# First MLP of a three-layer hybrid block: 17 of 22 pairs of up-projection tiles by seven block products

## The chip, the cores and the metric

One NeuronCore of a Trainium2 chip runs the whole program in one launch. The metric is the device time of an execution in microseconds (us); three runs of the kernel before gave 1718.68, 1718.99 and 1719.04 us, median 1718.99.

## What is computed

The reference runs a hybrid layer (gated linear attention beside sliding-window attention, then an MLP) and then two further layers, each an attention and an MLP, on 512 tokens of width 1024, in float32. The change touches the MLP of the first layer alone:

```
h2 = rms_norm(x, ffn_norm)                       # 512 x 1024
u = causal_dwconv(h2 @ w_up, conv_w, conv_b)     # w_up 1024 x 5632, three taps along the tokens
a, bval = jnp.split(u, 2, axis=-1)               # 2816 columns each
return x + (jax.nn.silu(a) * bval) @ w_down      # w_down 2816 x 1024
```

## The kernel before

Activations lie transposed: 128 features on the partitions, 512 tokens along the free axis. Every float32 product is made of three passes in a rounded format (fp32r): a value is split into a rounded "hi" (a copy by ACT) and the remainder "lo" (a subtraction), and hi x hi, hi x lo and lo x hi are summed in PSUM.

The up projection has 22 pairs of output tiles. A pair is one 128-column tile of `a` (p_ = 0) and its partner of `bval` (p_ = 1). A tile (`up_tile`, lines 1027 to 1038) is 8 chunks of the inner dimension by 3 passes, 24 matmuls of 128x512. Weights come by SyncE's queue as 128x1024 tiles into `stage`; ACT writes `w_hi` (`split_hi`, line 1506), GpSimd (POOL) writes `w_lo` in four operations of 128x256 (`split_lo`, line 507); each has two buffers. The evacuation of a tile runs on DVE and ACT in turn: DVE scales the bank by `rstd` (L2445), ACT starts the convolution (L1767), DVE adds the two other taps (L2447, L2450); after the first tile of a pair ACT takes the silu (L1770), after the second DVE multiplies (L2455) and the result is split at once into `f1_hi` (ACT, L1772) and `f1_lo` (DVE, L2458). The pairs rotate over four banks. The down projection (L1080 to L1086) then runs over `d`, the eight output tiles, each over all 22 tiles `f` in order; it reads `f1_hi` and `f1_lo` from the arena, which holds all 44 of them.

The later MLPs do their down projection already by seven products (`product`, L1444 to L1453) for each 2x2 group of weight blocks, a "quad": raw blocks land by DMA, ACT makes the hi parts (L2031), POOL and DVE the lo parts (L549, L2848), DVE the sums of weight blocks (L2830 to L2842) and the additions of the products (L2890). A product is 4 chunks by 3 passes, 12 matmuls of 128x256.

Each engine works its own program in order; a waiting instruction holds all that stand behind it. Orders are written out by hand.

Of the kernel before, what the change touches and what calls it, by code (L numbers as in the profile page):

```python
# [21 lines left out]
P = 128  # L22
# [28 lines left out]
N_UP1 = 2 * NF1  # L51
# [33 lines left out]
N_FC = 2 * KD * N_CH  # L85

# [46 lines left out]
def program(nc, x_in, params, consts, buckets, swa_table, weights, pairs, tables, out):  # L133
    with ExitStack() as ctx:
# [15 lines left out]
        with nc.sbuf_tensor("y", [P, 2, KD, HS], F32) as y:  # L150
            pass
        xn_hi = sb("xn_hi", [P, KD, S], F32R)
# [4 lines left out]
        with nc.sbuf_tensor("ff_space", [P, 2 * KD, S], F32) as early_space:  # L157
            with nc.sbuf_tensor("z", [P, N_IN, S], F32) as z, nc.sbuf_tensor("qkv", [P, 2, 3, S], F32) as qkv, \
                    nc.sbuf_tensor("prob", [P, 2, 2, S], F32) as prob, \
                    nc.sbuf_tensor("v_tok", [P, 2, 2, NQ, P], F32) as v_tok:  # L160
                pass
        arena = sb("arena", [P, 2 * NF1, S], F32R)
        v_split = sb("v_split", [P, 2, 2, NQ, P], F32R)
        bias = sb("bias", [P, 2, 2, EXT])
        tmp = sb("tmp", [P, 4, S])
        rstd = sb("rstd", [P, S])
        rstd_h = sb("rstd_h", [P, S])
# [10 lines left out]
        f1_hi, f1_lo = arena[:, 0:NF1], arena[:, NF1:2 * NF1]  # L178
# [81 lines left out]
        up_scaled, down_done = sem("up_scaled"), sem("down_done")  # L260
# [64 lines left out]
        flat_bias = bias[:].rearrange("p a b c -> p (a b c)")  # L325
# [55 lines left out]
        def _(sp):  # L381
# [15 lines left out]
            def quad_load(q, r):  # L397

                if q >= 2:
                    sp.wait_ge(slot_low, 5 * (q - 2) + (LO_POOL[HI_S4] if r == 0 else LO_POOL[HI_A22]))  # L400
                sp.dma_start(quad_in[q % 2][r], pairs[2 * q + r]).then_inc(quad_full[q % 2], 16)

            def mlp2_loads(l):

                for n in range(N_CH):
                    t = T_MLP2[l] + KD * n
                    q = quad_at(l, n)
                    if n:
# [16 lines left out]
                if l == 0:  # L425
                    sp.wait_ge(slot_low, 5 * quad_at(1, 0))
# [46 lines left out]
            loads(T_MLP1 + 4, T_QKV[0])  # L473
# [27 lines left out]
        def _(pool):  # L501
# [44 lines left out]
            def quad_low(q, k, src):  # L546

                pool.wait_ge(slot_high, N_HIGH * q + k + 2)
# [43 lines left out]
            split_los(T_OUT + 6, T_MLP2[0])  # L592
# [47 lines left out]
        def _(pe):  # L640
# [386 lines left out]
            def up_tile(m, p_, bank, first=False):  # L1027

                pe.wait_ge(hi_ready, 2 * m + p_ + 1)
                for k in range(KD):  # L1030
                    if first:
                        pe.wait_ge(xn_ready, KD + k + 1)
                    pe.matmul(UP[bank][:], w_hi[:, p_, k], xn_hi[:, k], start=(k == 0), stop=False)  # L1033
                    mm = pe.matmul(UP[bank][:], w_hi[:, p_, k], xn_lo[:, k], start=False, stop=False)  # L1034
                mm.then_inc(hi_free, 1)
                pe.wait_ge(lo_ready, 2 * m + p_ + 1)
                for k in range(KD):
                    mm = pe.matmul(UP[bank][:], w_lo[:, p_, k], xn_hi[:, k], start=False, stop=(k == KD - 1))  # L1038
                mm.then_inc(tile_done, 1)

            m = T_MLP1 // 2
            pe.wait_ge(evac[0], m + WO_HALVES)
            up_tile(m, 0, 0, first=True)
# [5 lines left out]
            pe.wait_ge(evac[1], m + WO_HALVES)  # L1049
            up_tile(m, 1, 1)  # L1050
            up_tile(m + 1, 0, 2)
            up_tile(m + 1, 1, 3)
            with pe.Fori(1, NF1 // 2) as i:
                for j in range(2):
                    pe.wait_ge(ff_ready, 2 * i + j - 1)
                    up_tile(2 * i + (m + j), 0, 2 * j)
                    pe.wait_ge(conv_2, 4 * i + (2 * j - 2))
                    up_tile(2 * i + (m + j), 1, 2 * j + 1)

            for d in range(KD):  # L1060
# [6 lines left out]
                if d < 2:  # L1067
                    pe.wait_ge(ff_ready, NF1 - 1)
                    pe.wait_ge(conv_2, 2 * NF1 - 2)
                else:  # L1070
                    pe.wait_ge(evac[d % 2], T_MLP1 // 2 + WO_HALVES + d // 2)
                for s_, ks in pieces:
# [4 lines left out]
                    for k, f in ks:  # L1077
                        if d == 0 and f == NF1 - 1:
                            pe.wait_ge(ff_ready, NF1)
                        pe.matmul(G[d % 2][:], w_hi[:, p_, k], f1_hi[:, f], start=(f == 0), stop=False)  # L1080
                        mm = pe.matmul(G[d % 2][:], w_hi[:, p_, k], f1_lo[:, f], start=False, stop=False)  # L1081
# [2087 lines left out]
```

## Time and profile before

| | |
|---|---|
| median of the runs shown | 1718.99 us |
| the profiled execution's own time | 1718.6 us |
| its span in the trace | 1716.8 us |
| TensorE (PE) busy | 1704.7 us, 99% |
| DVE / ACT / POOL busy | 1061.0 / 868.3 / 963.1 us |
| granted TensorE clock | 0.999 |
| up projection, tile (1,0) to the first matmul of the down projection | 210.15 to 438.63 us |

Busy time is the time in which an engine's records run. Records of matmuls overlap, since they are pipelined, so the start-to-start distance is what one of them costs. On DVE, ACT and POOL too a record can end up to 0.1 us after the next one has begun; who waits for it by a semaphore waits for its end.

### The profile page before, as it was taken

The numbers are of one execution on the slowest core, as the hardware profiler recorded it, in microseconds if no ns is written. First come the engines' busy times: TensorE is split into PE (matmuls) and PEld (weight loads), VectorE is DVE, ScalarE is ACT, GpSimd is POOL, SyncE is SP. The second block draws the span as 40 slices with busy tenths as digits, with TensorE's granted clock in tenths as the row PEclk, the third lists the DMA queues.
The fourth block names the chain that finished last, engine by engine and source line by source line (L and its number), as shares of the span: only waits on it lengthen the run. The fifth ranks groups of instructions, "written<-read, shape, count | busy, mean of one in ns | idle before, by whom it ended". The sixth has DMA issues, their size and how long they took to land.

```text
span 1716.8 us, 27243 instructions
## 1 busy us (share of the span) xinstructions
PE 1704.7 (99%) x9425; PEld 1440.6 (84%) x9425; DVE 1061.0 (62%) x2084; ACT 868.3 (51%) x1498; POOL 963.1 (56%) x1095
## 2 busy tenths in 40 slices
PE   9999999999999999999999999999999999999998
PEld 7778888888888778888989898977777889898988
DVE  6875755555311455568757575867776676757576
ACT  5665555555322444435545444546655554545355
POOL 5543655555555434357666666755554665656666
PEclk9999999999999999999999999999999999999999
DMA  5221333332334322223323323233322242333332
GB/s 192 74 68 61 100 98 98 97 93 93 108 95 137 104 68 83 74 74 123 99 98 99 105 96 106 64 128 116 105 97 70 87 133 91 109 99 98 99 98 74
DMA packets 48662, 167.91 MB, mean 98 GB/s; under 512 B 5376, under 2 KB 6672, under 8 KB 48528
## 3 DMA queue, kind: packets, MB, share of 16 engines
q1 hardware_dynamic: 48272, 166.05, 30.2%
q8 instruction: 61, 1.00, 0.2%
q10 hardware_dynamic: 288, 0.52, 0.1%
q14 instruction: 41, 0.34, 0.1%
HBM read 164.31 MB, written 2.24 MB: 97 GB/s over the span
## 4 chain that ended last, share of the span: by engine, by line
PE 90%; DVE 6%; ACT 2%; issue 1%; DMA 0%; POOL 0%; SPq 0%; DVEq 0%; ACTq 0%
PE bank L736 18%; PE bank L1444 6%; PE bank L1453 6%; PE bank L1445 6%; PE bank L661 5%; PE bank L660 5%; PE bank L666 5%; PE bank L1033 5%; PE bank L1034 5%; PE bank L1038 5%; PE bank L754 3%; PE bank L760 3%; PE bank L755 3%; PE bank L1086 2%; PE bank L1081 2%; PE bank L1080 2%
## 5 line engine op out<-in xcount | busy, mean ns | idle before, releaser
L507 POOL TENSOR_TENSOR w_lo<-stage,w_hi 128x256 fp32r<-128x256 f32 x872 | 672.2, 803 | 571.7 <-ACT w_hi L1506 317.5
L1506 ACT ACTIVATE w_hi<-stage 128x1024 fp32r<-128x1024 f32 x218 | 229.4, 1052 | 200.9 <-PE bank L1081 54.7
L660 PE MATMUL bank<-xn_hi,w_hi 128*128 128x512 f32 x544 | 211.8, 389 | 0.0
L661 PE MATMUL bank<-xn_lo,w_hi 128*128 128x512 f32 x544 | 211.7, 389 | 0.0
L736 PE MATMUL bank<-xn_hi,w_hi 128*128 128x512 f32 x464 | 189.1, 407 | 0.0
L736 PE MATMUL bank<-xn_lo,w_hi 128*128 128x512 f32 x464 | 181.8, 392 | 0.0
L2890 DVE TENSOR_TENSOR x<-x,bank 128x256 f32<-128x256 f32 (+1 forms) x217 | 97.4, 455 | 89.3 <-PE bank L1453 86.6
L1453 PE MATMUL bank<-arena 128*128 128x256 f32 x896 | 146.6, 283 | 0.0
L1033 PE MATMUL bank<-xn_hi,w_hi 128*128 128x512 f32 x352 | 137.1, 389 | 0.0
L1034 PE MATMUL bank<-xn_lo,w_hi 128*128 128x512 f32 x352 | 136.9, 389 | 0.0
L666 PE MATMUL bank<-xn_hi,w_lo 128*128 128x512 f32 x544 | 135.0, 389 | 0.0
L1444 PE MATMUL bank<-arena 128*128 128x256 f32 x512 | 129.4, 284 | 1.3 <-DVE arena L2910 0.8
L1445 PE MATMUL bank<-arena 128*128 128x256 f32 x512 | 128.7, 283 | 0.0
L1453 PEld LDWEIGHTS bank<-arena 128*128 128x128 f32 x896 | 124.8, 192 | 0.0
L736 PE MATMUL bank<-xn_hi,w_lo 128*128 128x512 f32 x464 | 123.9, 399 | 0.0
L666 PEld LDWEIGHTS bank<-xn_hi,w_lo 128*128 128x128 f32 x544 | 102.1, 188 | 21.2
L661 PEld LDWEIGHTS bank<-xn_lo,w_hi 128*128 128x128 f32 x544 | 102.2, 188 | 21.1
L660 PEld LDWEIGHTS bank<-xn_hi,w_hi 128*128 128x128 f32 x544 | 102.1, 188 | 20.9
L2910 DVE TENSOR_TENSOR arena<-tmp,arena 128x256 fp32r<-128x256 f32 (+2 forms) x128 | 115.0, 917 | 3.8 <-ACT arena L2067 2.5
L736 PEld LDWEIGHTS bank<-xn_hi,w_hi 128*128 128x128 f32 x464 | 87.2, 188 | 25.2 <-issue 8.5
L736 PEld LDWEIGHTS bank<-xn_hi,w_lo 128*128 128x128 f32 x464 | 84.6, 188 | 22.8 <-issue 6.0
L736 PEld LDWEIGHTS bank<-xn_lo,w_hi 128*128 128x128 f32 x464 | 87.3, 188 | 16.0
(374 smaller groups left out, 3719.3 us busy)
## 6 DMA issues: line engine op xcount, KB each, us to landing
stage<-weights SPq DMA_DIRECT2D x219, 512.0 KB, 3.6
prob<-pairs SPq DMA_DIRECT2D x32, 512.0 KB, 3.6
stage<-pairs SPq DMA_DIRECT2D x32, 512.0 KB, 3.6
bias<-table SPq DMA_DIRECT2D x11, 896.0 KB, 6.4
out<-y SPq DMA_DIRECT2D x8, 256.0 KB, 2.2
x<-x_in SPq DMA_DIRECT2D x3, 512.0 KB, 7.6
bias<-swa_table SPq DMA_DIRECT2D x4, 256.0 KB, 4.4
con<-consts SPq DMA_DIRECT2D x1, 640.0 KB, 9.8
```

The costliest lines, as they stand in the source:

```text
L507: ins = nc.gpsimd.tensor_tensor(w_lo[:, p_, ks], stage[:, p_, ks], w_hi[:, p_, ks].bitcast(F32), ALU.subtract)
L660: pe.matmul(G[p_][:], w_hi[:, p_, k], hi[:, k], start=(first and k == ks[0]), stop=False)
L661: mm = pe.matmul(G[p_][:], w_hi[:, p_, k], lo[:, k], start=False, stop=False)
L666: mm = pe.matmul(G[p_][:], w_lo[:, p_, k], hi[:, k], start=False, stop=(last and k == ks[-1]))
L736: mm = pe.matmul(G[p_][:], (w_hi if i < 2 * KD else w_lo)[:, p_, k], (xn_lo if i < 2 * KD and i % 2 else xn_hi)[:, k], start=(i == 0), sto ...
L1033: pe.matmul(UP[bank][:], w_hi[:, p_, k], xn_hi[:, k], start=(k == 0), stop=False)
L1034: mm = pe.matmul(UP[bank][:], w_hi[:, p_, k], xn_lo[:, k], start=False, stop=False)
L1444: pe.matmul(region, w, fc_hi[:, i, f], start=(fresh and i == 0), stop=False, skip_group_check=True)
L1445: pe.matmul(region, w, fc_lo[:, i, f], start=False, stop=False, skip_group_check=True)
L1453: mm = pe.matmul(region, w, fc_hi[:, i, f], start=False, stop=(i == QUADS - 1), skip_group_check=True)
L1506: act.activation(w_hi[:, p_], stage[:, p_], ACT.Copy).then_inc(hi_ready, 1)
L2910: dve.tensor_tensor(fc_lo[:, i, a:b + 1].rearrange("p c s -> p (c s)"), src, fc_hi[:, i, a:b + 1].rearrange("p c s -> p (c s)").bitcast(F3 ...
```

## The change

The first 5 pairs stay as they are (`up_tile`). For the other 17, the two output tiles and the halves of the inner dimension make a 2x2 group of weight blocks A11, A12, A21, A22, and the halves of the inner dimension by the halves of the tokens a 2x2 group of activation blocks B. Seven products of sums of blocks give the pair: 7 x 12 matmuls of 128x256 in place of 2 x 24 of 128x512. The raw blocks of a pair come by two DMAs of 512 KB.

The 28 factor blocks (7 sums of B, for 4 chunks of the inner dimension, hi and lo) are made once, in four steps `factors(k)`, one after the first tile of each of the pairs 0 to 3. They take the arena's upper part. So the products f of the MLP (`f1`) stay unsplit in the lower part, and `f1_hi` and `f1_lo` are made at the end, when a factor's space is free. The multiplication `silu * b` moves from DVE to POOL. What was an ACT/DVE loop with register-indexed columns is written out.

```diff
@@ sizes
-N_UP1 = 2 * NF1
+N_PLAIN = 5
+Q_UP = NF1 - N_PLAIN
+UP_ORDER = [HI_A11, HI_S1, HI_A12, HI_S2, HI_S4, HI_A22, HI_S3]
+POOL_LOWS = [2, 5, 8, 11, 14, 17, 20]
+DVE_LOWS = [f for f in range(NF1) if f not in POOL_LOWS]
@@ POOL
+            for i in range(N_PLAIN - 1):
+                if i:
+                    f_made_of(i - 1)
+                split_lo(T_MLP1 // 2 + i + 1, 0)
+                factor_lows(i)
+                split_lo(T_MLP1 // 2 + i + 1, 1)
+            f_made_of(N_PLAIN - 2)
...
+            for q in range(Q_UP):
+                up_low(HI_S3, q)
...
+                    up_low(HI_A11, q + 1)
+                f_made_of(N_PLAIN + q - 1)
+                if q + 1 < Q_UP:
+                    for k in (HI_A12, HI_S4, HI_A22):
+                        up_low(k, q + 1)
+            split_lo(T_DOWN1 // 2, 0)
+            split_lo(T_DOWN1 // 2, 1)
+            f_low(POOL_LOWS[0])
+            f_low(POOL_LOWS[1])
+            f_made_of(NF1 - 1)
@@ TensorE, up_product(q, k)
...
+                elif k == HI_S2:
+                    pe.wait_ge(up_moved, moved_at(q, P1_COPY))
+                elif k == HI_S4:
+                    pe.wait_ge(up_moved, moved_at(q, P5_COPY))
@@ ACT
+            for i in range(N_PLAIN - 1):
+                split_hi(T_MLP1 // 2 + i + 1, 0)
+                conv_0_of(i, 0)
+                silu(i)
+                factor_highs(i)
+                split_hi(T_MLP1 // 2 + i + 1, 1)
+                conv_0_of(i, 1)
...
+            for q in range(Q_UP):
...
+                    u3_copied(q - 1)
+                silu(i - 1)
+                up_high(HI_S3, q)
+                p1_copied(q)
+                conv_0_of(i - 1, 1)
...
+                    up_high(HI_A11, q + 1)
...
+                p5_copied(q)
+                if more:
+                    up_high(HI_S1, q + 1)
+                    up_high(HI_A12, q + 1)
...
+                u2_copied(q)
+                if more:
+                    up_high(HI_S2, q + 1)
+                    up_high(HI_S4, q + 1)
...
+                conv_0_of(i, 0)
+                if more:
+                    up_high(HI_A22, q + 1)
@@ DVE
+            def factors(k):
+                dve.scalar_tensor_tensor(out=e[:, 0:S], in0=x[:, k], scalar=pcol("ffn_norm", k, k + 1), in1=rstd[:],
+                                         op0=ALU.mult, op1=ALU.mult)
+                dlink(dve.scalar_tensor_tensor(out=e[:, S:2 * S], in0=x[:, k + 4], scalar=pcol("ffn_norm", k + 4, k + 5), in1=rstd[:],
+                                               op0=ALU.mult, op1=ALU.mult))
+                dve.tensor_tensor(t1, b12, b11, ALU.subtract)
+                dlink(dve.tensor_tensor(t3, b22, b12, ALU.subtract))
+                dlink(dve.tensor_tensor(t2, b22, t1, ALU.subtract))
+                dve.tensor_tensor(t4, b21, t2, ALU.subtract).then_inc(factor_made, 1)
...
+                    ins = dve.tensor_tensor(SUM_Y[:], a2[:, 0:S], a2[:, S:], ALU.add)
...
+                    ins = dve.tensor_tensor(up_s3(q), a1[:, 0:S], a2[:, 0:S], ALU.subtract)
...
+            for i in range(N_PLAIN):
+                scaled(i, 0)
+                conv(i, 0)
+                if i < N_PLAIN - 1:
+                    factors(i)
+                    scaled(i, 1)
+                    conv(i, 1)
...
+            for q in range(Q_UP):
...
+                    c_1(q - 1)
...
+                if more:
+                    up_sum(q + 1, HI_S1)
+                    up_sum(q + 1, HI_S3)
+                    up_sum(q + 1, HI_S2)
+                conv(i - 1, 1)
+                c_00(q)
+                if more:
+                    up_sum(q + 1, HI_S4)
+                    up_sum_low(q + 1, HI_S1)
+                    up_sum_low(q + 1, HI_S2)
+                c_01(q)
+                conv(i, 0)
+            for f in DVE_LOWS[0:2]:
+                f_low(f)
+            c_1(Q_UP - 1)
+            conv(NF1 - 1, 1)
+            for f in DVE_LOWS[2:]:
+                f_low(f)
```

Helpers that the diff calls: `factor_highs(k)` on ACT makes the hi parts of a step's factors (one operation of 256, one of 1536 elements), `factor_lows(k)` on POOL the lo parts of four of them (one operation of 1024), DVE those of the other three (256 and 512). `c_00`, `c_01`, `c_1` on DVE add two products into half a bank each; `p1_copied`, `p5_copied`, `u2_copied`, `u3_copied` on ACT copy a product of 128x256 out of PSUM before TensorE adds to its region or writes it anew.

## Rows read from the trace of the kernel before

**Rows 1.** The profile's first page: span, busy time, and the chain that ended last.
```profile
span 1716.8 us, 27243 instructions
PE 1704.7 (99%) x9425; PEld 1440.6 (84%) x9425; DVE 1061.0 (62%) x2084; ACT 868.3 (51%) x1498; POOL 963.1 (56%) x1095
...
PE 90%; DVE 6%; ACT 2%; issue 1%; DMA 0%; POOL 0%; SPq 0%; DVEq 0%; ACTq 0%
```

**Rows 2.** Windows: stretch and length, busy us of each engine (records), clock, DMA.
```profile
210.10:438.60 228.50, 228.50 (x1009) 189.20 (x1009) 119.59 (x168) 125.16 (x148) 119.12 (x169) 1.00 0.31 97
834.60:865.00 30.40, 30.40 (x256) 30.40 (x255) 19.32 (x37) 13.85 (x24) 18.14 (x15) 1.00 0.33 105
```

**Rows 3.** Timeline of PE, up projection: start, us, engine, line, operands, count.
```profile
210.15 0.39 PE L1033 MATMUL bank<-xn_hi,w_hi 128*128 128x512 f32 x1
...
431.37 1.98 PE L1038 MATMUL bank<-xn_hi,w_lo 128*128 128x512 f32 x8
433.19 0.39 PE L1033 MATMUL bank<-xn_hi,w_hi 128*128 128x512 f32 x1
...
438.63 0.39 PE L1080 MATMUL bank<-arena,w_hi 128*128 128x512 f32 x1
```

**Rows 4.** Timeline of PE, a later MLP's quads: first matmuls of two products.
```profile
850.56 0.28 PE L1444 MATMUL bank<-arena,v_split 128*128 128x256 f32 x1
850.68 0.28 PE L1445 MATMUL bank<-arena,v_split 128*128 128x256 f32 x1
...
852.00 0.28 PE L1444 MATMUL bank<-arena 128*128 128x256 f32 x1
```

**Rows 5.** Timeline of DVE, 198 to 206.5 us.
```profile
198.37 0.97 DVE L2337 TENSOR_TENSOR tmp<-tmp 128x512 f32<-128x512 f32 x1
199.26 1.23 DVE L2340 SCALAR_TENSOR_TENSOR xn_lo<-x,par,xn_hi 128x512 fp32r<-128x512 f32 x1
200.41 1.22 DVE L2337 TENSOR_TENSOR tmp<-tmp 128x512 f32<-128x512 f32 x1
202.33 0.69 DVE L2316 TENSOR_TENSOR arena<-tmp,arena 128x512 fp32r<-128x512 f32 x1 [0.70 <-ACT arena L1511]
...
206.28 0.69 DVE L2445 TENSOR_TENSOR bank<-bank,rstd 128x512 f32<-128x512 f32 x1
```

**Rows 6.** Timeline of POOL, 198 to 221 us.
```profile
198.05 4.18 POOL L507 TENSOR_TENSOR w_lo<-stage,w_hi 128x256 fp32r<-128x256 f32 x4 [1.12 <-ACT w_hi L1506]
207.57 2.83 POOL L507 TENSOR_TENSOR w_lo<-stage,w_hi 128x256 fp32r<-128x256 f32 x4 [5.34 <-ACT w_hi L1506]
```

**Rows 7.** Timeline of all engines from 196 us: convolution under POOL.
```profile
208.25 0.75 DVE L2447 SCALAR_TENSOR_TENSOR tmp<-bank,par,tmp 128x511 f32<-128x511 f32 x1 [1.28 <-ACT tmp L1767]
```

**Rows 8.** Timeline of DVE, 846 to 868 us.
```profile
851.10 0.68 DVE L2834 TENSOR_TENSOR qkv<-stage,bank 128x512 f32<-128x512 f32 x1
851.81 0.70 DVE L2837 TENSOR_TENSOR bank<-bank,stage 128x512 f32<-128x512 f32 x1
852.42 0.41 DVE L2890 TENSOR_TENSOR x<-x,bank 128x256 f32<-128x256 f32 x1
852.75 0.68 DVE L2842 TENSOR_TENSOR v_tok<-stage,bank 128x512 f32<-128x512 f32 x1
```

**Rows 9.** Timeline of ACT, same stretch.
```profile
852.55 0.60 ACT L2031 ACTIVATE v_split<-bank 128x512 fp32r<-128x512 f32 x1 [2.60 <-DVE bank L2837]
853.04 0.62 ACT L2031 ACTIVATE v_split<-stage 128x512 fp32r<-128x512 f32 x1
```

**Rows 10.** Timeline of POOL, same stretch.
```profile
857.29 1.29 POOL L549 TENSOR_TENSOR arena<-qkv,arena 128x512 fp32r<-128x512 f32 x1
```

**Rows 11.** Groups of ACT by form, 808 to 868 us: busy, mean ns, idle before.
```profile
L1506 ACT ACTIVATE w_hi<-stage 128x1024 fp32r<-128x1024 f32 x4 | 4.2, 1053 | 5.2 <-DMA stage<-weights 5.2
L2067 ACT ACTIVATE arena<-tmp 128x768 fp32r<-128x768 f32 x3 | 2.5, 848 | 4.4 <-DVE tmp L2935 4.4
L2059 ACT ACTIVATE arena<-tmp 128x256 fp32r<-128x256 f32 x2 | 0.8, 418 | 0.1
```

**Rows 12.** Timeline of ACT from 204 us.
```profile
205.06 1.28 ACT L1506 ACT_TABLE_LOAD   x1
...
211.41 0.76 ACT L1767 ACTIVATE tmp<-bank,par 128x512 f32<-128x512 f32 x1
```

More of the change, by code:

```diff
@@ L151, in program @@
             pass
+        with nc.sbuf_tensor("xn_raw", [P, 2 * KD, S], F32) as xn_raw:
+            pass
         xn_hi = sb("xn_hi", [P, KD, S], F32R)
@@ L166, in program @@
         rstd = sb("rstd", [P, S])
+        with nc.sbuf_tensor("rstd_slot", [P, S], F32R) as rstd_slot:
+            pass
         rstd_h = sb("rstd_h", [P, S])
@@ L1044, in _ @@
+            pe.wait_ge(evac[0], T_MLP1 // 2 + WO_HALVES)
+            up_tile(0, 0)
             norm(1)
@@ L1048, in _ @@
             mm.then_inc(tab_mm, 1)
[L1049 to L1058, printed above, removed]
+            pe.wait_ge(evac[1], T_MLP1 // 2 + WO_HALVES)
+            up_tile(0, 1)
+            for i in range(1, N_PLAIN):
+                for p_ in range(2):
+                    up_tile(i, p_)
+            for q in range(Q_UP):
+                for k in UP_ORDER:
+                    up_product(q, k)
             for d in range(KD):
@@ L1085, in _ @@
                     for k, f in ks:
-                        mm = pe.matmul(G[d % 2][:], w_lo[:, p_, k], f1_hi[:, f], start=False, stop=(f == NF1 - 1))
+                        mm = pe.matmul(G[d % 2][:], w_lo[:, p_, k], f1_hi[f], start=False, stop=(f == NF1 - 1))
                     if ends:
@@ L1774, in _ @@
+            f_high(2)
+            f_high(3)
+            u3_copied(Q_UP - 1)
+            silu(NF1 - 1)
+            f_high(4)
+            conv_0_of(NF1 - 1, 1)
+            for f in range(5, 14):
+                f_high(f)
+            split_hi(T_DOWN1 // 2 + 1, 0)
+            for f in range(14, NF1):
+                f_high(f)
             load_exp_and_ln()
-            n_split = 2
+            n_split = 3
             for d in range(KD):
@@ new lines, in _ @@
+            for q in range(Q_UP):
+                i, more = N_PLAIN + q, q + 1 < Q_UP
+                if q:
+                    c_1(q - 1)
+                else:
+                    scaled(i - 1, 1)
+                if more:
[4 more added lines that the diff above has]
+                c_00(q)
+                if more:
+                    up_sum(q + 1, HI_S4)
[3 more added lines that the diff above has]
+                conv(i, 0)
```

437 lines of the change are left out of this document (342 added, 95 removed).

## The prediction

> **What bounds the kernel now.** I read the first page, then the windows, then the timelines. TensorE is busy for 99% of the span and is 90% of the chain that ended last [rows 1]. In the up projection it has no idle time at all: 228.5 us busy in a window of 228.5, while DVE, ACT and POOL are at 120, 125 and 119 us [rows 2]. So a saved matmul is saved time as long as the others keep up, and any wait that reaches TensorE is lost time at full price.
>
> **What TensorE saves.** Eight matmuls of 128x512 take 433.19 - 431.37 = 1.82 us, 0.227 each, so a tile of 24 takes 5.44 and a pair 10.88; 21 pairs by that are 228.5, the distance between the first and the last row of the group [rows 3]. A product of 12 matmuls of 128x256 takes 852.00 - 850.56 = 1.44 us, 0.120 per matmul [rows 4]; seven are 10.08. The change saves 0.80 us in each of 17 pairs: -13.7 us. The columns fall by an eighth, the time by only 7%, because a short matmul costs more than half a long one. Everything else in the change can only cost.
>
> **The wait that I look for.** A DVE operation with two inputs in SBUF takes 0.69 us of 512 elements when POOL is idle and 1.22 or 1.23 us when POOL runs its subtractions [rows 5]; POOL's own four then take 4.18 us in place of 2.83 [rows 6]. The pattern is turns: one DVE and one POOL operation per 1.15 us (199.26 to 200.41). With a PSUM input DVE is not touched: 0.75 us within POOL's 207.57 to 210.40 [rows 6, 7]. So in a contest I charge 0.5 us for a DVE operation of 512 elements, 0.25 for 256, and for POOL 0.62 per 256 elements and 1.2 per 512 (0.09 below the record of 1.29 [rows 10]). The Trainium skill (SBUF — State Buffer, section "Who interferes with whom") states the same as a rule: DVE with two SBUF inputs and a GpSimd instruction that reads SBUF exclude each other, whichever starts first holds the ports for its whole instruction. By that rule a POOL operation of 1024 elements would hold DVE for all of its length, some 2.4 us as an estimate; the sum below doesn't use that.
> The old up projection has no such DVE operation: its products and remainders have a bank as one input. The new one adds many: the factors, their lo parts, two of four weight sums, and all lo parts of f.
>
> **Plain pairs 0 to 4.** One pair of this stage is a loop through three engines. POOL: f_made(i-1) 1.3, split_lo of the next first tile 2.8 [rows 6, 10]. DVE: factors(i), two operations of 512 and four of 256, some dependent: 3.1 alone. ACT: hi parts, 0.33 and 1.48 (256 to 1024 elements go from 0.42 to 1.05, so 0.21 per 256 more [rows 11]), 1.9 with handovers. POOL: factor_lows, 1024 elements at 0.59 per 256 plus start, 2.45, and only then split_lo for the second tile, 2.8. ACT's split_hi for that tile stands behind its hi parts likewise.
> Without turns, POOL's loop is 1.3 + 2.6 (rest of the factors) + 1.9 + 2.5 + 2.8 = 11.1 us, DVE's loop (two evacuations of 2.98, factors 3.1, hi parts 1.9, a remainder 0.6) 11.6, both over the 10.88 of a pair. The first evacuation starts at 206.28 [rows 5], so lo of tile (1,1) is there at about 220.2, while TensorE wants it at 210.15 + 9.07 = 219.2: 1.0 lost, then 0.5 to 0.7 per pair: 2.9 us in all, the lower end.
> With turns, factors(i) meets the four operations of split_lo: 0.5+0.62+0.5+0.62+0.25+0.62+0.25+0.62, then two dependent ones 0.9: 4.9 in place of 2.6, and DVE's remainder goes ahead of factor_lows for 0.5. The loop becomes 1.3 + 4.9 + 1.9 + 0.5 + 2.5 + 2.8 = 13.9, 3.0 over a pair, for pairs 2, 3 and 4: 1.0 + 9.0 = 10 us. The sums of the first quad then meet the last split_lo: +0.9. I take 11, since the turns are what the nearest rows show. Table loads (1.28 [rows 12]) go from twice per two pairs to once; they are hidden either way.
>
> **Hand-over to the quads.** Before the first S2 ACT must copy A11's product, behind the evacuation of pair 4, which DVE begins only after six sums and remainders; before the first S4 come the sums of the next quad and a convolution. Adding the durations below from the end of the last tile, S2 waits 0.2 and S4 1.5: 1.7 us.
>
> **A quad in steady state.** Durations, with what a successor on the same engine sees in brackets: DVE 512 0.69 (0.60), dependent 0.71, 256 0.42 (0.33) [rows 8]; ACT 0.62 (0.52), from a bank 0.60 (0.49), a copy of 256 0.42 (0.30) [rows 9, 11]; handover 0.04 (852.51 to 852.55 [rows 8, 9]); first tap 0.76 [rows 12], others 0.75 [rows 7]. Totals are some 8.4 us on DVE, 7.6 on ACT, 7.8 on POOL (six of 1.3), all under 10.08. But order counts, so I follow the loop that closes: from the end of conv(i-1,1): p5 copy, highs of S1 and A12, u2 copy, high of S2: 2.2; low of S2 0.6; c_01 0.42; first tap 0.77; two taps and on 1.44; c_1 0.67; sums S1, S3, S2 1.9; two taps 1.53; handovers 0.25. That is 9.8, 0.3 under 10.08: TensorE sets the pace, barely. Sums S1 and S3 are the two with both inputs in SBUF, 0.6 us each from about 1.3 us into the quad, and POOL's lo of S3 becomes ready at about 1.75, just there. If POOL gets its turn between them the loop is 9.8 + 1.15 = 11.0 and S4 waits 0.6; the next quad, which starts with DVE late, is then ahead of POOL and clean. Between 0 and 0.9 per quad (the loop of 11.0 each time), over 15 quads 0 to 13.5; I take 0.2 each, every third quad hit: 3 us.
> The raw blocks are asked for a whole quad ahead. DMA moves what it moved before; I charge nothing.
>
> **The start of the down projection.** Before, f is split as it comes. Now TensorE needs hi and lo of f in order while they are made. f0 and f1 are ready near the end of the last product (T). f2 is POOL's and stands behind two split_lo (5.7 us). f3 stands on DVE behind c_1(16) and conv(21,1): after T come 0.2, u3 copy 0.4, c_1 1.1, first tap 0.8, taps 1.5: T+4.3. Thirteen DVE remainders from there at 0.60: f21 at T+12.1. TensorE's order is hi of eight f's (0.45 each), then their w_lo pass (0.23 each), so it ends d = 0 at T+18.5 against 22 x 0.68 = 15.0: +3.5, lower end. With turns, POOL still has five remainders and eight operations of split_lo: 5 x (0.5 + 1.2) + 8 x 1.15 = 17.7 from about T+6.2: f21 at T+24, end at T+25.7: +10.7. I take 10, for a few will miss each other.
>
> **Sum.** -13.7 + 11 + 1.7 + 3 + 10 = +12.0 us on the profiled execution's 1718.6, whose span is 1716.8 and which lies 0.4 under the median of the runs: 1730.6, and 1731 against the median of 1718.99.
>
> **Rivals.**
> (1) No turns. If DVE's factor and remainder operations ran beside POOL, the lower ends hold: -13.7 + 2.9 + 1.7 + 0 + 3.5 = -5.6, 1713 us: faster. The place is the first four pairs and the stretch after T; it decides once the excess of a factor operation under POOL falls below some 0.2 us. For it: half of such pairs in a trace may simply not overlap in time. Against: rows 5 and 6 show exactly these kinds of operation at 1.22. Chance 13%.
> (2) The turns bite in one of the two places only, since the queues slide past each other: -13.7 + 11 + 1.7 + 0 + 3.5 = +2.5, or with the roles changed -13.7 + 2.9 + 1.7 + 1.5 + 10 = +2.4: 1721. Chance 17%.
> (3) The quad loop is the bound: 0.8 us over in each of 15 quads, 12 in place of 3: +21, 1740. It takes only 0.3 us more in that loop than I counted, or POOL's turn each time. Against it: the loop corrects itself once DVE is late. Chance 15%.
> The Trainium skill (TensorE: Matmul & The Clock Gate, section "HAM oscillation — how this bites in real kernels") warns that gaps in a matmul stream bring the half clock back. The granted clock is 1.00 in both windows here [rows 2], where no gaps are, so no row tells. As a mechanism of this kernel: after T TensorE would be busy 15 of 26 us, and if it fell from 2.4 to 1.2 GHz for 10 of these, work of some 6 us would double while the supply, not the clock, sets most of it: about +3, 1734. Chance 5%.
>
> **How the numbers follow.** Forecast 50%, with a range of its own of 1724 to 1738. Rivals (1) 13%, (2) 17%, (3) 15%, the clock 5%. The measurement tells 0.2%, 3.4 us, from no change. Faster needs under 1715.5: most of (1), 12%. Within: the rest of (1), half of (2), a little of the forecast's low edge: 12%. Slower 76%. The range that leaves out no more than two in ten is 1715 to 1742.
>
> **What would show it.** Right: PE idle before L1038's counterpart in the second tiles of pairs 2 to 4, released by POOL's w_lo, about 3 us per pair, and TensorE's matmuls of the factors starting near 265 us; DVE's factor operations of 512 at 1.1 us and more, POOL's w_lo in these pairs above 0.8; quads 10.1 to 10.4 us apart, with waits at S4 on ACT's copy if any; after the last product some 10 us of PE idle released by DVE's and POOL's remainders. Wrong: quads farther than 10.8 apart (3), no idle PE in pairs 2 to 4 (1), or a cost after the down projection has started, which I have at none.

## The result and the profile after

Four runs of the changed kernel gave 1733.16 to 1735.41 us, median 1733.77; the kernel before, on the same chip, 1718.84. The ratio is 1.0089 with a 95% interval of 1.0073 to 1.0105: slower, 2.8 us over the forecast of 1731. The profiled execution took 1733.16 us, its span 1731.1 against 1716.8 [rows 1]: 14.3 us more.

The first page, with busy time in us, share of the span and instructions by engine:

```profile
span 1731.1 us, 28394 instructions
PE 1700.6 (98%) x10037; PEld 1460.6 (84%) x10037; DVE 1144.6 (66%) x2223; ACT 898.6 (52%) x1638; POOL 1039.9 (60%) x1077
```

TensorE has less to do and the span is longer. The windows of the changed stage (stretch, length, then busy us of PE, PEld, DVE, ACT and POOL, granted clock, DMA share, GB/s) stand against a stretch that was full before [rows 2]:

```profile
197.50:265.00 67.50, 59.45 (x252) 45.92 (x251) 50.16 (x71) 31.82 (x41) 49.73 (x46) 0.99 0.27 91
265.00:440.00 175.00, 170.63 (x1403) 169.11 (x1402) 143.40 (x230) 119.86 (x236) 136.74 (x103) 1.00 0.28 99
440.00:480.00 40.00, 33.80 (x147) 25.86 (x147) 22.62 (x26) 20.94 (x33) 30.32 (x31) 0.91 0.22 72
```

Some 8 us are missing in the plain pairs, 4 in the quads, 6 at the start of the down projection. What ended TensorE's waits in the whole stretch from 197 to 480 us (engine, line, what it waited for: us in total, times, longest):

```profile
PE bank L1225 <- ACT bank L2003: 4.4, 8, 0.7
PE bank L1190 <- POOL w_lo L600: 4.3, 4, 1.9
PE bank L1185 <- ACT w_hi L1701: 3.8, 3, 1.3
PE bank L1275 <- DVE arena L2836: 2.9, 4, 1.2
PE bank L1275 <- POOL arena L708: 2.8, 2, 1.7
PE bank L1275 <- ACT arena L2021: 0.5, 1, 0.5
```

L1185 and L1190 are a plain tile's matmuls (hi and lo of the weights), L1225 a product's, L1275 the down projection's; L2003 is the copy of S4's bank. Idle time taken by distance from start to start, less the distance of matmuls in a full stream, is a little more than the waits say: 0.93 in pair 1, 2.67 in pair 2, 2.67 in pair 3, 3.66 in pair 4, together 9.9; 6.1 in eight quads; 9.7 at the start of the down projection, its half clock included. The matmuls saved are 17 x 0.804 = 13.7.

**The plain pairs.** The timeline (start, us, engine, line, operands, count, idle before and releaser), one pair:

```profile
219.97 1.30 POOL L703 TENSOR_TENSOR arena_raw<-tmp 128x512 f32<-128x512 f32 x1
220.88 0.95 DVE L2765 SCALAR_TENSOR_TENSOR arena_raw<-x,par,rstd 128x512 f32<-128x512 f32 x1
221.21 4.11 POOL L600 TENSOR_TENSOR w_lo<-stage,w_hi 128x256 fp32r<-128x256 f32 x4
221.75 1.22 DVE L2767 SCALAR_TENSOR_TENSOR arena_raw<-x,par,rstd 128x512 f32<-128x512 f32 x1
...
225.64 0.43 DVE L2772 TENSOR_TENSOR arena_raw<-arena_raw 128x256 f32<-128x256 f32 x1
...
227.97 2.90 POOL L689 TENSOR_TENSOR arena<-arena_raw,arena 128x1024 fp32r<-128x1024 f32 x1 [2.65 <-ACT arena L1975]
230.84 2.81 POOL L600 TENSOR_TENSOR w_lo<-stage,w_hi 128x256 fp32r<-128x256 f32 x4
233.70 2.12 PE L1190 MATMUL bank<-xn_hi,w_lo 128*128 128x512 f32 x8 [0.88 <-POOL w_lo L600]
...
234.51 0.93 DVE L2765 SCALAR_TENSOR_TENSOR arena_raw<-x,par,rstd 128x512 f32<-128x512 f32 x1
```

The six factor operations (220.88 to 226.07) take 5.2 us beside POOL's four subtractions, which take 4.11 in place of 2.81. In step 0, where POOL is idle, the same six take 3.1 (209.31 to 212.42). From factor to factor DVE needs 234.51 - 220.88 = 13.6 us, a pair of tiles 10.88.

**The quads.** The groups of 265 to 430 us by form (line, engine, operands, count | busy us, mean ns of one | idle before) show the turns as two kinds of one instruction. L2791 is the sum S3 and L697 POOL's lo parts; the blocks of every second quad lie in `xn_raw`, those of the others in `stage`:

```profile
L697 POOL TENSOR_TENSOR rstd_slot<-xn_raw,bias_slots 128x512 fp32r<-128x512 f32 x15 | 23.7, 1578 | 13.5 <-ACT bias_slots L1991 13.5
L2791 DVE TENSOR_TENSOR xn_raw<-xn_raw 128x512 f32<-128x512 f32 x8 | 14.3, 1790 | 0.0
L2791 DVE TENSOR_TENSOR xn_raw<-stage 128x512 f32<-128x512 f32 x8 | 5.5, 685 | 0.0
```

Eight sums at 1.79, eight at 0.69: every second quad S3 waits for a whole operation of POOL. What follows, in one quad that is hit:

```profile
277.64 1.79 DVE L2791 TENSOR_TENSOR xn_raw<-xn_raw 128x512 f32<-128x512 f32 x1
...
280.85 0.75 DVE L2753 SCALAR_TENSOR_TENSOR tmp<-bank,par,tmp 128x510 f32<-128x510 f32 x1
281.69 0.37 ACT L2003 ACTIVATE bank<-bank 128x256 f32<-128x256 f32 x1 [2.72 <-DVE tmp L2753]
...
282.21 0.36 PE L1225 MATMUL bank<-arena,bias_slots 128*128 128x256 f32 x1 [0.65 <-ACT bank L2003]
```

The sum delays the two taps, these ACT's copy, and the copy the first matmul of S4: 0.81 us lost in the first such quad, about 0.7 in each later one, none in the quads between. Two quads take 20.91 us against 2 x 10.08.

**The start of the down projection.** DVE's and POOL's timelines from 446 us:

```profile
447.95 8.39 DVE L2836 TENSOR_TENSOR arena<-arena_raw,arena 128x512 fp32r<-128x512 f32 x8
...
448.30 1.73 POOL L703 TENSOR_TENSOR xn_raw<-tmp 128x512 f32<-128x512 f32 x1
```

Eight remainders of f take 8.39 us, 1.05 each, where 0.60 is the distance without POOL.

**The clock.** Windows around the two places where TensorE is interrupted:

```profile
260.00:264.00 4.00, 2.14 (x8) 1.72 (x8) 3.61 (x6) 2.12 (x4) 4.00 (x5) 0.87 0.27 75
264.00:268.00 4.00, 4.00 (x24) 3.81 (x24) 3.12 (x6) 2.07 (x4) 2.90 (x4) 0.70 0.48 187
...
448.00:452.00 4.00, 2.47 (x5) 1.63 (x6) 4.00 (x4) 3.15 (x7) 4.00 (x4) 0.50 0.08 31
```

A granted clock of 0.50 is the lower level, 1.2 GHz. The last three matmuls of the plain stage start 0.43 us apart in place of 0.23, and the first nine of the first product 0.21 in place of 0.12; 1.6 us go by in this way. Whether they cost anything is taken up under "Hand-over".

### The profile page after: what moved, and what is told of

It is laid out like the page before. It is cut to its first block, busy times and chain, and to the rows that moved or that the text cites. A ratio compares the mean times of both kernels' runs of the same rounds, so it can differ in the third digit from the quotient of the medians.

```text
span 1731.1 us, 28394 instructions
## 1 busy us (share of the span) xinstructions
PE 1700.6 (98%) x10037; PEld 1460.6 (84%) x10037; DVE 1144.6 (66%) x2223; ACT 898.6 (52%) x1638; POOL 1039.9 (60%) x1077
## 4 chain that ended last, share of the span: by engine, by line
PE 85%; DVE 7%; POOL 3%; ACT 3%; issue 2%; DMA 0%; SPq 0%; DVEq 0%; ACTq 0%; POOLq 0%
PE bank L885 18%; PE bank L1639 6%; PE bank L1648 6%; PE bank L1640 6%; PE bank L810 5%; PE bank L809 5%; PE bank L815 5%; PE bank L1225 3%; PE bank L1226 3%; PE bank L1233 3%; PE bank L903 3%; PE bank L909 3%; PE bank L904 3%; PE bank L1275 2%; PE bank L1276 2%
## 5 line engine op out<-in xcount | busy, mean ns | idle before, releaser
L600 POOL TENSOR_TENSOR w_lo<-stage,w_hi 128x256 fp32r<-128x256 f32 x736 | 582.9, 823 | 455.2 <-ACT w_hi L1701 222.2
L1701 ACT ACTIVATE w_hi<-stage 128x1024 fp32r<-128x1024 f32 x184 | 193.7, 1053 | 202.0 <-PE bank L1276 56.7
L810 PE MATMUL bank<-xn_lo,w_hi 128*128 128x512 f32 x544 | 211.7, 389 | 0.0
L809 PE MATMUL bank<-xn_hi,w_hi 128*128 128x512 f32 x544 | 211.7, 389 | 0.0
L885 PE MATMUL bank<-xn_hi,w_hi 128*128 128x512 f32 x464 | 189.0, 407 | 0.0
L885 PE MATMUL bank<-xn_lo,w_hi 128*128 128x512 f32 x464 | 181.8, 392 | 0.0
L1648 PEld LDWEIGHTS bank<-arena 128*128 128x128 f32 x896 | 124.8, 192 | 0.0
L1639 PEld LDWEIGHTS bank<-arena 128*128 128x128 f32 x512 | 98.2, 192 | 2.8 <-issue 2.7
L1640 PEld LDWEIGHTS bank<-arena 128*128 128x128 f32 x512 | 98.2, 192 | 0.0
```

The lines of the kernel that those rows point to most:

```text
L600: ins = nc.gpsimd.tensor_tensor(w_lo[:, p_, ks], stage[:, p_, ks], w_hi[:, p_, ks].bitcast(F32), ALU.subtract)
L809: pe.matmul(G[p_][:], w_hi[:, p_, k], hi[:, k], start=(first and k == ks[0]), stop=False)
L810: mm = pe.matmul(G[p_][:], w_hi[:, p_, k], lo[:, k], start=False, stop=False)
L885: mm = pe.matmul(G[p_][:], (w_hi if i < 2 * KD else w_lo)[:, p_, k], (xn_lo if i < 2 * KD and i % 2 else xn_hi)[:, k], start=(i == 0), sto ...
L1639: pe.matmul(region, w, fc_hi[:, i, f], start=(fresh and i == 0), stop=False, skip_group_check=True)
L1640: pe.matmul(region, w, fc_lo[:, i, f], start=False, stop=False, skip_group_check=True)
```

## The experiments

Each ratio is to the kernel before, measured on the same chip. Waits are those of one profiled execution of each kernel. "The changed kernel" is the one above, 1733.77 us.

### One part alone

**1. Order of the split.** POOL and ACT split the next tile before they make the factors' parts.

```diff
-                factor_lows(i)
                 split_lo(T_MLP1 // 2 + i + 1, 1)
+                factor_lows(i)
...
-                factor_highs(i)
                 split_hi(T_MLP1 // 2 + i + 1, 1)
+                factor_highs(i)
```

> In plain pairs 0 to 3, POOL's split_lo and ACT's split_hi of the next second tile go ahead of the factors' lo and hi parts; nothing else moves. Turns and order together (my theory): in the changed kernel TensorE loses 0.9, 2.7, 2.7 and 3.7 us in pairs 1 to 4 plus about 1.6 at half clock. With the splits ahead no tile waits, but DVE's own loop, with turns some 13.4 us per pair, still makes the last factors late, so the first product waits near 256 us in place of starting at 264.6: the time falls by 6 to 9 us, to about 1726. Rival, turns alone: the same operations meet on DVE and POOL whatever the order, the loop stays 13.6 us per pair, and the first product still starts at 263 us or later: under 2 us gained.

Measured: 1737.37 us (1735.86 to 1738.21), ratio 1.0108 [1.0091, 1.0125]: 3.6 more than the changed kernel, where 6 to 9 less were expected. TensorE's waits:

```profile
PE bank L1233 <- POOL v_split L697: 3.2, 1, 3.2
...
PE bank L1190 <- POOL w_lo L600: 2.7, 2, 1.4
...
PE bank L1225 <- ACT rstd L1996: 1.5, 1, 1.5
```

The plain tiles did gain: their waits fell from 8.1 to 4.6 us (2.7 at L1190, 1.9 at L1185). But POOL's splits now form one series of eight, `factors` meets it from end to end (DVE's pass is 236.10 - 221.81 = 14.3 us in place of 13.6), and the quads start short of A11's lo part (3.2) and of the first copy (L1996). The wait was moved over the hand-over and grew on the way. My claim that the order was the fault fell.

**2. Factor operations without a second SBUF input.** All six read their second input from an idle bank. Instructions, sizes and order are the same; the factors then hold other values than they should, so only the time is read.

```diff
-  ..., scalar=pcol("ffn_norm", k, k + 1), in1=rstd[:],
+  ..., scalar=pcol("ffn_norm", k, k + 1), in1=SUM_X[:],
...
-                dve.tensor_tensor(t1, b12, b11, ALU.subtract)
+                dve.tensor_tensor(t1, b12, SUM_X[:, 0:HS], ALU.subtract)
```

> The six DVE operations that make a step's factors read their second input from an idle PSUM bank in place of SBUF, at the same sizes and in the same order; the factors hold other values than they should. Turns (my theory): DVE's operations fall from 1.22 and 0.85 to 0.75 and 0.43 us, POOL's four of split_lo from 4.1 to 2.8, the loop of a pair from 13.6 to 11.3, TensorE's loss before the first product from 11 to about 3, half clock gone: 7 to 9 us faster, about 1726. Rival, order alone: the chain of factors, hi parts, lo parts and split sets the pace at whatever length, DVE's durations don't fall, no more than 2 us gained.

Measured: 1726.92 us (1726.64 to 1727.30), ratio 1.0048 [1.0031, 1.0065]: 6.9 less; 7 to 9 were expected. The operations of 512 take 0.74 us and those of 256 0.42, POOL's four 2.84 to 2.86, and DVE's pass falls to 232.08 - 220.54 = 11.5 us (11.6 in the prediction's sum without turns). In the waits the plain pairs' fell from 8.1 to 2.7, and the first wait of the hand-over appeared, 1.3 of the 5.0:

```profile
PE bank L1225 <- ACT bank L2003: 5.0, 8, 1.3
...
PE bank L1190 <- POOL w_lo L600: 2.7, 4, 1.3
```

**3. POOL out of the way of S3.** POOL's first lo part of a quad waits until DVE has made the next quad's S3.

```diff
+                if 0 < q < Q_UP - 1:
+                    pool.wait_ge(sum_made, N_SUM * (q + 1) + UP_SUM[HI_S3])
                 up_low(HI_S3, q)
```

> In every quad but the first and the last POOL's lo part of S3 waits until DVE has made sum S3 of the next quad; same work. Turns (my theory): the 0.76 us at S4 in every second quad come from POOL's operation between sums S1 and S3, and nothing needs that lo part before 9.6 us into the quad; all quads come to 10.08 us, 6 us gained, about 1728. Rival, DVE's and ACT's loop is too long by itself: the waits at S4 stay, within 1 us of the changed kernel, or slower for the added wait.

Measured: 1727.72 us (1727.07 to 1727.86), ratio 1.0051 [1.0034, 1.0068]: 6.0 less. The same sum by form, and the one wait for the copy that is left:

```profile
L2793 DVE TENSOR_TENSOR xn_raw<-stage 128x512 f32<-128x512 f32 x8 | 5.5, 684 | 0.0
L2793 DVE TENSOR_TENSOR xn_raw<-xn_raw 128x512 f32<-128x512 f32 x8 | 5.5, 684 | 0.0
```

```profile
PE bank L1227 <- ACT bank L2005: 1.3, 1, 1.3
```

Both forms take 0.684, every steady-state wait of the quads is gone, the plain waits are as they were (4.3 and 3.8). POOL's delay costs nothing in the quads. Since the form that took 1.79 us now takes 0.684, its buffer was not the cause.

**4. Remainders of f without a second SBUF input.** DVE's 15 lo parts of f read a bank in place of `f1_hi`; the lo parts then hold other values than they should.

```diff
-  dve.tensor_tensor(f1_lo[f], f1[f], f1_hi[f].bitcast(F32), ALU.subtract)...
+  dve.tensor_tensor(f1_lo[f]..., f1[f]..., SC[1][:, HS:S]....broadcast_to([P, 2, HS]), ALU.subtract)...
```

> DVE's fifteen lo parts of f read their second input from an idle half of a PSUM bank, read twice, in place of SBUF; the lo parts hold other values. Turns (my theory): they fall from about 1.2 to 0.75 us, POOL's remainders and splits run unhindered, the loss at the start of the down projection falls from 9.7 to about 4 us: 5 to 6 us faster, about 1728. Rival, order alone (f2 behind two splits on POOL, f3 behind the last additions on DVE): at most 1.5 us gained.

Measured: 1727.34 us (1727.15 to 1728.33), ratio 1.0052 [1.0035, 1.0069]: 6.4 less; 5 to 6 were expected. The waits at L1275 fell from 6.2 us to 2.3 on DVE and 0.8 on POOL; by the distance of starts TensorE lost about 4 us there in place of 9.7, and the granted clock is 1.00 in all windows from 440 to 464. So of the 5.7 gained by starts 3.1 is waits, and up to 2.6 goes with the clock, which no longer falls; how much of that the clock itself is worth is not shown:

```profile
448.00:452.00 4.00, 3.76 (x16) 2.94 (x17) 4.00 (x8) 3.60 (x8) 3.56 (x3) 1.00 0.00 0
```

### The same without changing a value

**5. Factors through banks.** `rstd` is copied to a bank once, B12 is made in a bank; four of six operations then have one bank as input, T2 and T4 do not.

```diff
+                if k == 0:
+                    dlink(dve.tensor_copy(SUM_X[:], rstd[:]))
+                b12 = OB[:, 0:HS]
+                for h, o in ((0, b11), (1, b12)):
+                    dve.scalar_tensor_tensor(out=o, in0=x[:, k, h * HS:(h + 1) * HS], ...
+                                             in1=SUM_X[:, h * HS:(h + 1) * HS], ...)
```

> Full computation. rstd is copied once into an idle bank and B12 is made straight in another, so that four of the six kinds of factor operation have one PSUM input; only T2 and T4 (256 elements each, dependent) still have two SBUF inputs. Turns (my theory): the loop of a plain pair falls from 13.6 to about 11.8 us, TensorE's loss before the first product from 11 to about 4: 6 to 8 us faster than the changed kernel, about 1727, as with the factors read from a bank. Rival, that run gained by its other values and not by the ports: no more than 2 us gained.

Measured: 1731.04 us (1729.92 to 1731.65), ratio 1.0071 [1.0055, 1.0088]: 2.7 less, not the 6 to 8 expected, and not the 2 or less of the rival either; its time alone does not decide. The trace does: T4, which still has two SBUF inputs, takes 0.84 us in place of 0.42 in 2, B12 is an operation more, DVE's pass is 233.84 - 221.75 = 12.1 us, between the 11.5 of 2 and the 13.6 of the changed kernel, and the waits of the plain pairs are 4.7 us, between 2.7 and 8.1. The less of the contention an edit removes, the less it gains, with right values or wrong ones.

**6. The end on DVE alone.** All 22 lo parts of f on DVE, four of them already in the last quad.

```diff
-POOL_LOWS = [2, 5, 8, 11, 14, 17, 20]
+POOL_LOWS = []
...
+                else:
+                    for f in range(4):
+                        f_low(f)
                 c_01(q)
```

> Full computation. All 22 lo parts of f on DVE, four of them already in the last quad between c_00 and c_01, hi parts 0 to 3 ahead on ACT; POOL keeps the splits of the down weights. Port and supply (my theory): the shared port is asked for 22 x 0.5 + 16 x 0.62 = 21 us in place of 26, and 4 of the 22 are done before the last product ends; the loss at the start of the down projection falls from 9.7 to about 5 us, 1729. Rival, the last evacuation (c_1, two taps) and what stands behind it sets the pace: within 1.5 us of the changed kernel.

Measured: 1731.92 us (1729.59 to 1732.89), ratio 1.0073 [1.0056, 1.0090]: 1.9 less. Some 5 were expected, and 1.5 or less by the rival. The waits at the start of the down projection fell from 6.2 to 3.4 us, but 1.3 appeared at the hand-over, which this edit doesn't touch (`L1219 <- ACT L1997`, longest 1.3 in place of 0.7; see "Hand-over" below).

The profiled execution shows why the time gained so little. The first matmul of the attention behind this MLP starts at 558.31 us in the kernel before, at 572.69 in the changed one (14.4 later) and at 569.10 here (10.8 later): the stage gained 3.6 us. But from the start of the last matmul to the end of the span it takes 8.9 us in place of 6.9: the transfers of the output pause for some 1.5 us there. No edit touches that place, and the profiled executions of 8 and 12 have the same 2 us; all others have 6.9. So 3.6 is the better measure of this edit.

**7. 3, 5 and 6 together.**

> Full computation; the three edits at once: factors in banks, POOL's lo of S3 waiting for the sum, f's lo parts on DVE. If the three losses are separate places, as my theory has it, the gains add: 7 + 6 + 5 = 18 us, 1716, which is 3 us under the kernel before. Rival, a loss taken away in one place comes back at the next (the hand-over to the quads above all): 1720 to 1724.

Measured: 1720.77 us (1719.72 to 1722.49, ten runs), ratio 1.0012 [1.0002, 1.0021]: 13.0 less than the changed kernel. No quad waits at all. What is left:

```profile
PE bank L1186 <- POOL w_lo L600: 4.5, 4, 1.8
PE bank L1271 <- DVE arena L2837: 2.5, 2, 1.3
PE bank L1271 <- ACT arena L2017: 1.0, 1, 1.0
```

### What is left

Five more went for the last 2 us, in the plain pairs and at the end.

**8. 7 with the order of 1.**

> The three edits, and the splits of the next second tile ahead of the factors' hi and lo parts, as in the first run. My theory of that run's loss: there all DVE operations of a step met eight POOL operations, DVE's loop was 14.3 us and the late evacuations were paid in the first quads. With the factors in banks few meet, so here the order should pay: 1 to 3 us under the run without it, 1714. Rival, the order itself is bad, since it makes the last factors and the first quad late: 2 to 4 us over it.

Measured: 1722.11 us (1720.52 to 1724.98), ratio 1.0016 [1.0007, 1.0026]: 1.3 more than 7, in ranges that overlap. The gain of 1 to 3 us failed, and the rival (2 to 4 over) was right in its direction. In the profiled execution, the slowest of the ten, the waits moved to the first quad as in 1:

```profile
PE bank L1221 <- ACT rstd L1992: 2.9, 1, 2.9
PE bank L1229 <- POOL v_split L697: 2.8, 1, 2.8
```

**9. 7 with both seams tightened.** DVE scales the second tile before it makes the factors' lo parts, the last quad's hi and lo parts of f come one or two earlier, and POOL's last product goes ahead of the second split of the down weights.

```diff
                 dve.tensor_tensor(t4, b21, t2, ALU.subtract).then_inc(factor_made, 1)
+                scaled(k, 1)
...
+                if not more:
+                    f_low(4)
                 conv(i, 0)
-            f_low(4)
-            c_1(Q_UP - 1)
             f_low(5)
+            c_1(Q_UP - 1)
+            f_low(6)
```

> Full computation; the three edits and two of order: DVE scales the second tile of a plain pair between the factors and their lo parts, where it waited for ACT; in the last quad f4 to f7 are split earlier, POOL's f_made(21) goes ahead of the second split of the down weights, and ACT's split_hi of that tile behind f7. The run with three edits still lost 1.05, 1.1, 1.05 and 2.0 us in the plain pairs, 4.3 us at f4 to f7 and some 3 us at half clock. My theory: DVE's loop of 12.1 us per plain pair falls to 11.4 and f4 to f7 come in time, together 4 to 6 us less, 1716, 2 to 4 under the kernel before. Rival, DVE and POOL still meet for as long and the waits only move to f8 and later: 1719 to 1721.

Measured: 1720.70 us (1719.87 to 1722.20, eleven runs), ratio 1.0011 [1.0002, 1.0020]; not told apart from 7. The waits on w_lo are unchanged (4.5 in all). DVE's timeline shows where the earlier scaling went:

```profile
225.29 0.69 DVE L2742 TENSOR_TENSOR bank<-bank,rstd 128x512 f32<-128x512 f32 x1
...
227.23 0.69 DVE L2781 TENSOR_TENSOR arena<-arena_raw,arena 128x512 fp32r<-128x512 f32 x1 [0.93 <-ACT arena L1971]
228.84 0.75 DVE L2749 SCALAR_TENSOR_TENSOR tmp<-bank,par,tmp 128x511 f32<-128x511 f32 x1 [0.92 <-ACT tmp L1958]
```

DVE scales at 225.29, but still idles 0.93 for ACT's hi parts and 0.92 for the convolution: factor to factor takes 233.28 - 221.21 = 12.07 us, in 7 it is 12.10.

**10. 9 with the first quad's sums after the last split.**

```diff
+                    dve.wait_ge(lo_ready, T_MLP1 + 2 * N_PLAIN)
```

> As the run before it, and DVE's sums for the first quad wait until POOL has split the last plain tile. My theory: the 2.0 us lost at the last plain tile, 0.9 of them by turns with sums S1 and S3, become 1.1, and the sums themselves are 1 us shorter: 1 us gained. Rival: the first quad's sums come 1 to 2 us later and TensorE waits for them in that quad: 1 to 2 us lost.

Measured: 1726.81 us (1725.86 to 1727.70), ratio 1.0044 [1.0030, 1.0058]: 6.1 more than 9. The longest wait on w_lo fell from 1.8 to 0.9, and the first quads paid 1.2 + 3.1 (`L1221 <- ACT v_split` and `L1221 <- ACT rstd`). The rival held in its direction; it had put the loss at 1 to 2 us.

**11. 7 with POOL's product between the split and the factors' lo parts.**

```diff
+                split_lo(T_MLP1 // 2 + i + 1, 0)
                 if i:
                     f_made_of(i - 1)
-                split_lo(T_MLP1 // 2 + i + 1, 0)
```

> Full computation: the three edits, and in plain pairs 1 to 3 POOL multiplies silu by b (f_made, 1.28 us) after the split of the first tile, in the 2.2 us in which it waits for ACT's factors, not ahead of the split. With the run that scaled the second tile earlier and gained nothing, I now hold that POOL's own chain sets the 12.1 us of a plain pair: f_made 1.28, split with turns 3.1, ACT 2.0, factor_lows 2.9, split 2.8. Then this edit takes 1.2 off: the waits of 1.05 at the second tiles go, 3 us gained on the run with three edits, 1717 to 1718. Rival, DVE's loop is the bound: the waits stay, under 1 us gained.

Measured: 1721.70 us (1719.97 to 1723.13, eleven runs), ratio 1.0016 [1.0007, 1.0025]: the expectation of 1717 to 1718 failed. One pass of DVE and POOL:

```profile
221.84 0.47 DVE L2766 SCALAR_TENSOR_TENSOR arena_raw<-x,par,bank 128x256 f32<-128x256 f32 x1
...
223.71 1.30 POOL L703 TENSOR_TENSOR arena_raw<-tmp 128x512 f32<-128x512 f32 x1
...
224.18 1.10 DVE L2772 TENSOR_TENSOR arena_raw<-arena_raw 128x256 f32<-128x256 f32 x1
...
227.65 2.90 POOL L689 TENSOR_TENSOR arena<-arena_raw,arena 128x1024 fp32r<-128x1024 f32 x1 [2.65 <-ACT arena L1971]
...
234.19 0.47 DVE L2766 SCALAR_TENSOR_TENSOR arena_raw<-x,par,bank 128x256 f32<-128x256 f32 x1
```

POOL still idles 2.65 us before L689, so its order can't be what binds. From 221.84 to 234.19 is 12.35, and all of it is on DVE: factors, two stops for ACT's hi parts, two evacuations of 2.98. POOL's product now falls on T2 (1.10 in place of 0.42) and makes the pass 0.25 longer than in 7.

**12. 11 with the end of 9, and POOL's splits of the third and fourth down tile held back.**

```diff
+            split_lo(T_DOWN1 // 2, 1)
+            pool.wait_ge(ff_ready, FF_PREP + 16)
             split_lo(T_DOWN1 // 2 + 1, 0)
+            pool.wait_ge(ff_ready, FF_PREP + NF1)
             split_lo(T_DOWN1 // 2 + 1, 1)
```

> Full computation: as the run before it, with the tighter last quad, and POOL holds back the splits of the third and fourth down tile until DVE has made 16 and 22 lo parts of f. In the run with the tighter last quad each f from f9 on came 1.14 us after the one before it, one DVE and one POOL turn. My theory: without these eight POOL operations DVE delivers one per 0.6 us and the loss at the start of the down projection falls from some 6 to 3 us: 1714 to 1715, 4 us under the kernel before. Rival, the splits themselves are then late for TensorE: 1717 or more.

Measured: 1721.90 us (1720.38 to 1722.39, eleven runs), ratio 1.0014 [1.0005, 1.0023]: the expected 1714 to 1715 failed too. The attention behind the MLP starts 1.6 us later than in the kernel before, in 11 as in 12: the edit gained nothing. The split that could not be held back, the second down tile's, now lies in the middle of DVE's series:

```profile
438.58 8.76 DVE L2841 TENSOR_TENSOR arena<-arena_raw,arena 128x512 fp32r<-128x512 f32 x9
...
440.38 4.61 POOL L600 TENSOR_TENSOR w_lo<-stage,w_hi 128x256 fp32r<-128x256 f32 x4
```

Nine remainders take 8.76 us; in 11 ten took 7.20. TensorE's waits there are 3.6 us on DVE's remainders; in 11 they are 2.4 on these and 1.0 on ACT's hi parts, about the same.

None of the twelve beats the kernel before. The best, 7 and 9, are 0.1% above it, with intervals that just leave out equality.

## Why the prediction was right, point by point

**The saving.** Predicted -13.7, found -13.7: quads that wait for nothing are 10.08 us long.

**Plain pairs.** Predicted 11, found 9.9 (the 1.6 at half clock behind them belongs to the hand-over, below). The turns are shown by 2: the same instructions with one input in a bank cost 6.9 us less. The places were right: waits in the second tiles of pairs 2 to 4, POOL's subtractions above 0.8, factor operations of 512 at 0.93 to 1.22, the first product at 264.6 ("near 265"). The loop was named half right. I priced POOL's at 13.9 with turns and stopped adding DVE's at 11.6 without; DVE's measures 13.6, and the trace and 11 show that it is the one that closes: POOL idles 2.65 us in each pass, waiting through ACT for DVE's factors, and reordering POOL gains nothing. The size did not suffer, since the 2.3 us of turns that I added to POOL's sum make DVE's 13.9 as well. With most turns gone DVE's pass is 12.1, still above the 10.88 of a pair: by the distance of starts 7 still loses 8.1 us up to the end of the first quad and 6.0 at the start of the down projection, together a little more than the 13.7 saved. Experiments 1, 8 and 11 rearranged POOL's or ACT's queue around a loop that was on DVE.

**Hand-over.** Predicted 1.7 (S2 waits 0.2, S4 1.5), found about that, but in two guises. In the changed kernel no wait stands at the first quad's S4; TensorE reaches it late, by the 1.6 us at half clock. In 3 and 6, where the plain pairs have the same waits but the clock stays at 1.00, S2 starts 0.2 late and S4 1.5. The two rows of S4's first matmul, the changed kernel's and then 6's, and 6's windows:

```profile
271.25 0.35 PE L1225 MATMUL bank<-arena,bias_slots 128*128 128x256 f32 x1
...
271.34 0.36 PE L1219 MATMUL bank<-arena,bias_slots 128*128 128x256 f32 x1 [1.30 <-ACT bank L1997]
```

```profile
260.00:264.00 4.00, 2.13 (x10) 1.65 (x10) 3.62 (x6) 2.13 (x4) 4.00 (x5) 1.00 0.25 68
264.00:268.00 4.00, 4.00 (x35) 4.00 (x34) 3.12 (x6) 1.98 (x4) 2.98 (x3) 1.00 0.49 195
```

S4 starts at the same time, for ACT's copy ahead of it ends at 271.10 us in one and at 271.20 in the other. So the half clock at this place cost nothing of its own: it filled a wait that was there. All profiled executions but 1, 8 and 10, whose first quads wait elsewhere too, fall into the two kinds: the half clock and no such wait in the changed kernel, 4, 5 and 7; the clock at 1.00 and the wait of 1.3 us in 2, 3, 6, 9, 11 and 12. Why the clock falls in one and not in the other is open: in the changed kernel and in 6 TensorE's waits before it are the same to 0.1 us.

**Quads.** Predicted 3 (every third quad), found 6.1. This is the mis-sized step: a quad that is hit lets only the next one go clean, not the next two, and each costs 0.76, not 0.6. It makes up the 2.3 us that the sum was short, and more. That the wait is S3's turn with POOL's lo part is shown by 3, which keeps these two apart and takes away 6.0 us. The chain I followed was right to within that: loop 9.8 + 1.1 against 10.08.

**Start of the down projection.** Predicted 10, found 9.7. Without a second SBUF input on DVE's remainders (4) it is about 4, near the lower end of 3.5.

**The sum.** -13.7 + 9.9 + 1.8 + 6.1 + 9.7 = +13.8, with 1.8 for the hand-over (1.6 at half clock and 0.2 at S4); measured in the span +14.3. The 0.5 left lies in the same stretch, since the attention behind it already starts 14.4 us later; forecast was +12.0. The range held the time with room; the terms were off by -1.1, +3.1 and -0.3, so that a part of the miss in the quads was offset by luck.

**The rivals.** "No turns" (1713) is refuted by 2, 3 and 4, each 6 to 7 us. "In one place only" (1721) too: they are in all three. "The quad loop is the bound" (12 in the quads) took half its price. The half clock, which I gave 5% and put at the end alone, did occur, in both places: at the first it took the place of the hand-over's wait, and at the second, by experiment 4, it is at most some 2.6 of the 9.7 (5.7 gained by the distance of starts, 3.1 of it waits). It may be less: in 9 and 12 the clock is 1.00 throughout the start of the down projection, which still loses 7.3 and 6.3 us, while 6 and 7, at 0.52 to 0.63 for a while, lose 7.1 and 6.0. The Trainium skill (TensorE: Matmul & The Clock Gate, section "HAM oscillation — how this bites in real kernels") describes the clock falling after waits of several us in each loop of a kernel; here no single wait of TensorE is over 1.9 us, and the granted clock is 0.50 in 448 to 452 all the same. But in 12, with a stretch as thin (2.59 and 2.68 us busy in 438 to 442 and 442 to 446), it stayed at 1.00. What makes it fall was not told apart.

**What adds up and what doesn't.** Edits 3, 5 and 6 alone gave 6.0, 2.7 and 1.9, together 13.0, more than their sum of 10.6. Most of the difference is not the edits': by the start of the attention behind the MLP, which leaves out the 2 us at the end of 6, they gave 5.8, 3.7 and 3.6, and together 13.9, against a sum of 13.0. The 0.9 that is left goes with the start of the down projection, which loses 7.1 us in 6 and 6.0 in 7; why is not shown.

## What to carry to other kernels

Seven products in place of eight save an eighth of the columns, but here only 7% of a pair's matmul time, 13.7 us in all, against which every factor, sum and remainder on the other engines must be hidden, at both seams as well as in steady state. Where GpSimd is busy, count a DVE operation with two SBUF inputs at its own length plus up to one operation of GpSimd (here 0.69 became 1.22 us beside operations of 256 elements and 1.79 beside those of 512), give it a PSUM operand if a bank is free, or make one of the two wait for the other where there is slack: one such wait gave back 6 us. Time a single stage by the start of what follows it, too: the 2 us at the very end of its profiled execution hid half of what experiment 6 gained. And before reordering a queue that TensorE waits for, follow the loop until it closes: if the engine named in the wait idles inside it, the order of that engine is not the lever.

## What the runs showed of the hardware

The turns go by whole instructions. The Trainium skill (SBUF — State Buffer, section "Who interferes with whom") says that a DVE instruction with two SBUF inputs contends with a GpSimd instruction that reads SBUF; the trace agrees, with 1.79 us against 0.69 for the same subtraction. What I had not expected is how it locks onto a rhythm: of the 16 sums S3 the 8 of one form are all slow and the 8 of the other all clean, and a mean over all (1.24) would show neither. It is a rhythm and not the buffer: in 2 and 6, where the first quad's S4 waits, the two forms have changed places (1.65 us from `stage`, 0.68 from `xn_raw`). My reading, which no run tests by itself, is that the delay of one quad moves DVE past POOL in the next.

A fallen clock does not have to cost time. The nine matmuls of 128x256 at the start of the first product are 0.21 us apart, not 0.12, though no wait stands between them; but they only arrive later at a wait that 3 and 6 show in full. And the same waits of TensorE (up to 1.9 us, the same seven) were followed by the lower clock in the changed kernel and not in 3 and 6.
